# The two halves of each stationary weight laid side by side, element by element, in a float32 kernel with three products for one

## What is computed

```python
h = rms_norm(x, norm_mix_g[l])
proj = h @ w_in[l]
...
x = x + mix @ w_out[l]
...
x = x + peer_ffn(rms_norm(x, norm_ffn_g[l]), peer_w_q[l], peer_sub_keys[l], peer_u[l], peer_v[l])
...
h = h + conv_glu(rmsnorm(h, ffn_norm[i]), ffn_w_in[i], ffn_conv_w[i], ffn_conv_b[i], ffn_w_out[i])
```

## Time and profile before

| | |
|---|---|
| median of 3 runs | 2023.91 us |
| profiled execution, first to last instruction | 2021.6 us |
| TensorE matmul (PE) busy | 1877.1 us, 93% |
| TensorE weight load (PEld) busy | 1800.7 us, 89% |
| VectorE (DVE) busy | 1456.5 us, 72% |
| ScalarE (ACT) busy | 1242.6 us, 61% |
| DMA | 146 GB/s on average, 47.0% of the 16 engines' time |
| mean granted TensorE clock | 0.975 |

### The profile page before, as it was taken

One profiled execution on the slowest core, in us unless ns is written; L12 is line 12 of the kernel. 1 busy time (PEld: TensorE's weight loads), 2 busy tenths in 40 slices (PEclk: granted clock), 3 DMA queues, 4 the chain that ended last, 5 costly groups with the idle time before them and its releaser, 6 DMA issues. The chain is left out here.

```text
span 2021.6 us, 45016 instructions
## 1 busy us (share of the span) xinstructions
PE 1877.1 (93%) x16518; PEld 1800.7 (89%) x16518; DVE 1456.5 (72%) x3046; ACT 1242.6 (61%) x2420; POOL 0.2 (0%) x4
## 2 busy tenths in 40 slices
PE   8998988999999999999999989687999977999997
PEld 8887888999999976899999989587999976899996
DVE  7667667688985479766666667776888678578857
ACT  5454655777776789655555556733665555666555
POOL 0000000000000000000000000000000000000000
PEclk9999999999999999999999999798999989999998
DMA  6533344466655620266666646101665644166562
GB/s 208 158 97 105 118 143 136 132 194 193 179 186 175 186 84 0 84 194 190 196 191 193 193 139 199 52 3 56 184 196 173 192 126 136 34 190 189 176 198 76
DMA packets 102084, 296.06 MB, mean 146 GB/s; under 512 B 9539, under 2 KB 32454, under 8 KB 101830
## 3 DMA queue, kind: packets, MB, share of 16 engines
q1 hardware_dynamic: 101958, 294.35, 47.0%
HBM read 293.26 MB, written 1.05 MB: 146 GB/s over the span
## 5 line engine op out<-in xcount | busy, mean ns | idle before, releaser
L459 DVE TENSOR_TENSOR w_low<-ring,w_high 128x512 fp32r<-128x512 f32 x1102 | 743.2, 685 | 357.1 <-ACT w_high L453 349.2
L503 PE MATMUL bank<-a_high,w_high 128*128 128x256 f32 x3228 | 921.2, 285 | 74.3 <-DVE w_low L459 39.1
L504 PE MATMUL bank<-a_low,w_high 128*128 128x256 f32 x3228 | 907.5, 281 | 0.0
L505 PE MATMUL bank<-a_high,w_low 128*128 128x256 f32 x3228 | 907.4, 281 | 0.0
L453 ACT ACTIVATE w_high<-ring 128x512 fp32r<-128x512 f32 x1102 | 671.4, 624 | 375.3 <-PE bank L505 372.8
L503 PEld LDWEIGHTS bank<-a_high,w_high 128*128 128x128 f32 x3228 | 620.0, 192 | 90.0 <-DVE w_low L459 39.7
L504 PEld LDWEIGHTS bank<-a_low,w_high 128*128 128x128 f32 x3228 | 616.3, 191 | 0.4
L505 PEld LDWEIGHTS bank<-a_high,w_low 128*128 128x128 f32 x3228 | 616.7, 191 | 0.0
L503 PE MATMUL bank<-s_high,w_high 128*128 128x256 f32 x1024 | 283.5, 277 | 2.0 <-DVE s_low L2446 2.0
L504 PE MATMUL bank<-s_low,w_high 128*128 128x256 f32 x1024 | 283.3, 277 | 0.0
L505 PE MATMUL bank<-s_high,w_low 128*128 128x256 f32 x1024 | 283.3, 277 | 0.0
(11 more groups left out here) (368 smaller groups left out, 1867.8 us busy)
## 6 DMA issues: line engine op xcount, KB each, us to landing
ring<-in_stream SPq DMA_DIRECT2D x273, 512.0 KB, 3.7
ring<-in_peer_u SPq DMA_DIRECT2D x128, 512.0 KB, 3.6
ring<-in_peer_v SPq DMA_DIRECT2D x128, 512.0 KB, 3.5
ring<-in_stream SPq DMA_DIRECT2D x32, 256.0 KB, 3.3
ring<-in_stream SPq DMA_DIRECT2D x12, 192.0 KB, 2.7
x<-in_x SPq DMA_DIRECT2D x4, 256.0 KB, 6.3
arena<-in_mem SPq DMA_DIRECT2D x1, 1024.0 KB, 11.0
out<-x SPq DMA_DIRECT2D x4, 256.0 KB, 2.6
```

The lines of the kernel that those rows point to most:

```text
L459: self.nc.vector.tensor_tensor(self.cut(h, self.w_low), self.raw(h), self.cut(h, self.w_high.bitcast(F32)), ALU.subtract)\
L503: self.nc.tensor.matmul(to, lh, rh, start=start, stop=False, **more)
L504: self.nc.tensor.matmul(to, lh, rl, start=False, stop=False, **more)
L505: return self.nc.tensor.matmul(to, ll, rh, start=False, stop=stop, **more)
```

## The change

For weights that stand still, a high part and its low part now lie next to each other: high of element 0, low of element 0, high of element 1, and so on. A block's high parts are then 128 numbers 8 bytes apart, spread over 1024 bytes of each partition, and so are its low parts. One tile `w_both` of four slots x 1024 numbers takes the place of `w_high` and `w_low`; its size is the sum of theirs. For the four matrices whose weights move (`WIDE`), the first 512 numbers of the slot are the high parts and the last 512 the low parts, so that they are contiguous as before. The activations' tiles (`a_high`, `a_low`, `s_high`, `s_low`) are untouched. No instruction is added, removed or moved on any engine, and no semaphore changes: the four engines' lists read alike but for the tile's name and the line numbers (L453 becomes L453 with another view, L459 becomes L460, and L503 to L505 become L516 to L518).

```diff
-        self.w_high = sb("w_high", [P, SLOTS, HALF * P], F32R)
-        self.w_low = sb("w_low", [P, SLOTS, HALF * P], F32R)
+        self.w_both = sb("w_both", [P, SLOTS, 2 * HALF * P], F32R)
...
-        self.nc.scalar.activation(self.cut(h, self.w_high), self.raw(h), ACT.Copy)\
+        high, _ = self.split_parts(h)
+        self.nc.scalar.activation(self.cut(h, high), self.raw(h), ACT.Copy)\
             .then_inc(self.high, 1)
...
-        self.nc.vector.tensor_tensor(self.cut(h, self.w_low), self.raw(h),
-                                     self.cut(h, self.w_high.bitcast(F32)), ALU.subtract)\
+        high, low = self.split_parts(h)
+        self.nc.vector.tensor_tensor(self.cut(h, low), self.raw(h),
+                                     self.cut(h, high).bitcast(F32), ALU.subtract)\
             .then_inc(self.low, 1)
+
+    def split_parts(self, h):
+        both = self.w_both[:, h % SLOTS, :]
+        if self.wide(h // 2):
+            return both[:, 0:HALF * P], both[:, HALF * P:2 * HALF * P]
+        both = both.rearrange("p (f two) -> p f two", two=2)
+        return both[:, :, 0], both[:, :, 1]
...
+    def stretch(self, h, at):
+        high, low = self.split_parts(h)
+        return high[:, at], low[:, at]
+
     def block_of(self, pe, n):
         h = n // HALF
         if n % HALF == 0:
             pe.wait_ge(self.low, h + 1)
-        at = slice((n % HALF) * P, (n % HALF + 1) * P)
-        return self.w_high[:, h % SLOTS, at], self.w_low[:, h % SLOTS, at]
+        return self.stretch(h, slice((n % HALF) * P, (n % HALF + 1) * P))
```

More of the change, by code:

```diff
@@ L467, in cut @@
             f = 32 if odd else 64
-            return w[:, h % SLOTS, 0:BLK * f].rearrange("p (b f) -> p b f", f=f)
+            return w[:, 0:BLK * f].rearrange("p (b f) -> p b f", f=f)
         if self.of("mla_uk", g):
-            return w[:, h % SLOTS, 0:2 * P].rearrange("p (j i f) -> p j i f", i=2, f=64)
-        return w[:, h % SLOTS, :]
+            return w[:, 0:2 * P].rearrange("p (j i f) -> p j i f", i=2, f=64)
+        return w
     def raw(self, h):
@@ L496, in row_of @@
             pe.wait_ge(self.low, h + 1)
-        at = slice((n % HALF) * P, (n % HALF + count) * P)
-        return self.w_high[:, h % SLOTS, at], self.w_low[:, h % SLOTS, at]
+        return self.stretch(h, slice((n % HALF) * P, (n % HALF + count) * P))
     def three(self, to, pairs, start, stop, **more):
@@ L975, in on_pe @@
                             now = slice(m * P, (m + 1) * P)
-                            w = self.w_high[:, half_at % SLOTS, now], self.w_low[:, half_at % SLOTS, now]
+                            w = self.stretch(half_at, now)
                             to = self.bank[room[u + 1, 0] if odd else room[u, m // 2]]
@@ L2047, in turn @@
                                 ins = self.three(self.bank[k % 4][:, 0:T],
-                                                 ((self.w_high[:, h % SLOTS, s],
-                                                   self.w_low[:, h % SLOTS, s]),
+                                                 (self.stretch(h, s),
                                                   (self.a_high[:, c, :], self.a_low[:, c, :])),
@@ L2410, in turn @@
                                 opens = isinstance(it, int) and k == 0 and c % 2 == 0
-                                ins = self.three(to, ((self.w_high[:, h % SLOTS, s],
-                                                       self.w_low[:, h % SLOTS, s]),
+                                ins = self.three(to, (self.stretch(h, s),
                                                       (s_high[:, k % SIDES, :], s_low[:, k % SIDES, :])),
```

## The result

The changed kernel takes 2082.53 us (median of 4 runs, 2081.57 to 2083.25), the kernel before, on the same chip, 2025.79 us (median of 4, 2022.76 to 2031.83). The ratio is 1.0276, with a 95% interval of 1.0249 to 1.0303: slower by 2.8%. The prediction said 1995 us, in a range from 1965 to 2065. It was wrong in direction, and the time lies outside the range. The profiled execution spans 2080.2 us, 58.6 more than before.

A forecast was written before the change was run, and what follows sets the result against it. TensorE was taken to set the pace. Losing the slow pace (17 us) plus half of 30 us gave 32, less a tenth 29: 2021.6 - 29 = 1992.6, with 2.3 for timed runs 1995 us; range 1965 to 2065.

The forecast's parts named there:

- the control: Moving matmuls of 512 columns, whose layout is unchanged, should keep 230 ns.
- The load of the stationary weights: TensorE's stationary loads, now spanning 1024 bytes per partition in place of 512: no added cost taken.
- its own case: TensorE's matmuls with stationary weights get faster: 1995 us, own range 1982 to 2007, chance 0.50.
- The clash: Weight load and moving operand collide reading SBUF, costing 2, 7 or 15 ns depending on how they lie in time.
- the gain from equal sweeps: Both SBUF reads now sweep 1024 bytes per matmul and need not keep meeting: together 32 us, 29 after a tenth off.
- (a): In TensorE's slow stretches the slow pace goes: 3700 matmuls x 4.5 ns = 17 us gained.
- (b): All 12,756 stationary-weight matmuls pass from 113.3 towards the load's own 111 ns: 30 us gained, half taken.
- C: Every matmul with a stationary weight block: the clash grows, slower, 41 us (2065), or 191 (2215) at worst; chance 0.20.
- D: ScalarE's and VectorE's splits get longer: up to 240 us, or 47 us where TensorE already waits; chance 0.04.
- The cover: Per weight group, TensorE's 2.72 us of matmuls hide up to about 0.45 us more per ScalarE or VectorE split.
- B: Nothing happens, 2024 us: the 2 to 7 ns could be a handover between load and matmul inside TensorE; chance 0.22.
- E: Stationary loads last by the bytes spanned, 178 ns more in each of 12,756: up to 4290 us; chance 0.04.

The follow-up runs named there:

- the flat layout: The changed kernel with w_both kept, but each half's 512 high parts first and 512 low parts after, 4 bytes apart: 2028.3 us, ratio 0.9988 to the kernel before.

## Why the prediction was wrong

*Step by step.* That TensorE sets the pace and that the splitting follows was right: every loss is in TensorE's busy time, and the waits of the earlier trace rows kept their order. That no instruction is added or moved was right, and so was the control.

*"The load of the stationary weights ... I take nothing."* This is the step that failed first. The row named as the nearest, the contiguous float32 load, is nearest in elements and type, and not in what costs: the pieces of 16 bytes that are touched. By itself the load rose from 111.7 to 117.8 ns, and with 256 moving columns from 113.3 or 117.8 to 120.0. The bound above (4290 us, by bytes spanned) was far off on the other side, and the run with a 32-byte step shows why: span is nearly free, pieces are not. The prediction gave a load that stays at 188 ns as the sign of its own case; it went to 194 to 196, and these 6 to 8 ns are most likely the 6 ns of pace seen a second time.

*"The clash", and the gain from equal sweeps.* Nothing of the gain was seen. The slow pace did go, as (a) said, but upwards; (b) went the wrong way. The premise under it, that the moving stream alone has room to spare beside 113.3 ns, came from the earlier trace rows, where bf16 stood for float32 (512 columns in 215 ns, 108 for 256). The row that could have corrected it was there: 512 float32 columns take 230 ns, so 256 would take 115, between the two paces 113.3 and 117.8. By the run with both operands interleaved the moving float32 operand was itself at or near its limit, and the 15 ns over bf16 needed no clash. This is argued, and rough: 115 lies above the 113.3 that was measured. What makes the 2 ns (2 or 6 beside contiguous loads) that 256 moving columns add to the load's own pace, a clash or something else, no run tells.

*C, the rival that a load touches twice as many pieces, slower,* had the right place and the right quantity; that the pieces of 16 bytes are the unit is shown by the steps of 12, 16 and 32 bytes (176.7, 235.8, 242 ns). Its price was 41 us: the fast part of the matmuls from 113.3 to 117.8. The measured account is 63.0 of busy time. The term that was missing: all 12,756 matmuls went on to 120.0, 2.2 ns each, 28 us. Against that stands the mean before, 115.1 ns by the trace and not 114.6, which takes 6 us off: about a third of the matmuls were at the slow pace (4300, not 3700), and the rest of the difference is uneven steps. 41 + 28 - 6 = 63. C was held back to 0.20 by the sentence that "one step aside should settle it", for which no row stood.

*D, longer splits,* half true: ScalarE's split rose by 42 to 49 ns with the stepped write, where nothing had been taken. The row taken as the nearest, L2307, writes pieces of four numbers, which fill 16 bytes as contiguous ones do, and could not speak on a step of 8 bytes. The cover that was named for it (0.45 us per split) held, as the run with stepped writes alone shows at 0.9997. VectorE's rose by 1 ns.

*B* fell with the result, and so did *E*, which had every load 178 ns longer; the step of 32 bytes confirms it.

*What stays open.* Why the kernel before has two paces, and what decides between them; in the kept traces it never changes within a row of matmuls whose steps all stay under 126 ns. The 48 matmuls that move 256 columns of weights, whose loads stay contiguous in the changed kernel, still show one of the two: 117.8 ns before, 113.3 after. The runs of the kernel before spread from 2020 to 2048 us while the changed kernel's four lie within 2 us, and the two paces may have a part in that, but it is not shown: the profiled executions with the flat layout and with stepped writes alone span 2019.7 and 2031.3 us, and their mean steps, 115.2 and 115.3 ns, make 2 us of these 11.6. Why going from 16 to 32 bytes still costs 6 ns. The 5 us between the changed kernel and the run with stepped reads alone (2082.53, 2077.65), whose ranges overlap: the mean step is 120.1 ns in both traces, so they are not in the steady pace. The granted clock is 0.974 in one profiled execution and 0.981 in the other; whether ScalarE's longer splits are behind that was not tried. And whether a load that takes two or four neighbouring numbers at a time from a stepped tensor would be free again, which was not tried either.

## What to carry to other kernels

Where a float32 operand is read with a step, count the 16-byte pieces that it touches and set the 1.84 ns measured here (at a granted clock of 1.00) on each; if that comes near the pace that TensorE keeps now, the step is not free, and for the moving operand there was no room at all (453 ns in place of 230). A pace a few ns above what one stream should need is first to be compared with the other stream in its own type, before a clash is assumed. And an unknown cost should not be taken from the row that looks most like it, but bounded by the quantity that could carry it: elements, bytes spanned, or pieces touched give three different answers.

## What the runs showed of the hardware

- TensorE's float32 loads at a granted clock of 1.00, pace for 128 numbers: about 111.7 ns contiguous and 117.8 at a step of 8 bytes, both beside 16 moving columns (113.3 or 117.8, and 120.0, beside 256); 176.7 at 12, 235.8 at 16, 242 at 32, all three beside 256. The larger of some 111 and 1.84 ns times the pieces fits the first four within 1 ns.
- The same price fits the moving side: 512 columns contiguous are 128 pieces in 230 ns, 1.80 each, and 256 pieces in 453 ns, 1.77 each; 256 columns at the 8-byte step are 128 pieces in 229 ns, 1.79 each. For 256 contiguous columns (64 pieces) 1.77 to 1.84 ns make 113 to 118, where both paces of before lie. This last is a fit, not a test.
- At a granted clock of 0.50 a float32 load with 128 moving columns keeps a pace of 213 ns in either layout; at 1.00, with 128 columns beside it too, 111.8 contiguous and 118.6 at the step of 8 bytes.
- ScalarE's float32 write of 512 elements, 8 bytes apart, takes 666 to 673 ns in place of 624; VectorE's read and write so, 686 in place of 685.
- Two float32 matmuls and a bf16 one in turn take 363 ns, where three in float32 take 340; the bf16 load begins 0.24 us behind the float32 one before it.
